# RWKV stage of a two-block kernel: the finished outputs in one part behind the second first inverse on VectorE, the first low rank weights loaded during the projection, and the first tile's own order

## The reference, cut to what matters

```python
def rwkv7_scan(r, w, k, v, kk, a, S):
    """S_t = S_{t-1} (diag(w_t) - kk_t^T (a_t * kk_t)) + v_t^T k_t ;  y_t = S_t r_t."""

# rwkv_project
lw = einsum("zblr,zrd->zbld", tanh(einsum("bld,zdr->zblr", xw, w1)), w2) + w0
decay = exp(-exp(-softplus(-lw) - 0.5))
a = sigmoid(a0 + (xa @ a1) @ a2)
g = sigmoid(xg @ g1) @ g2
kk = k * kvec[0] / max(sqrt(sum over the head of (k * kvec[0])^2), 1e-12)
k = k * (1 + (a - 1) * kvec[1])

# rwkv_out
y = head_layernorm(y, lnx[0], lnx[1])
bonus = sum over the head of (r * k * kvec[2]) * v
return ((y + bonus) * g) @ w_o
```

## Time and profile before

| | us |
|---|---|
| median of 3 runs | 3209.08 (3206.1 to 3211.09) |
| the profiled execution, its own time | 3212.0 |
| its span, first to last instruction | 3210.0 |
| TensorE busy | 3044.9 (95%) |
| VectorE busy | 1132.0 (35%) |
| ScalarE busy | 586.4 (18%) |
| GpSimd busy | 230.5 (7%) |

### The profile page before, as it was taken

The page is one execution under the profiler, slowest core; times in us unless marked ns, Lnnn a source line. Parts: engine busy times, 40 slices in busy tenths (PEclk is TensorE's granted clock), DMA queues, the critical chain, the costliest instruction groups (busy, mean ns, idle before and its releaser), DMA issues. The chain is left out here.

```text
span 3210.0 us, 54308 instructions
## 1 busy us (share of the span) xinstructions
PE 3044.9 (95%) x24038; PEld 1845.4 (57%) x24038; DVE 1132.0 (35%) x2357; ACT 586.4 (18%) x1323; POOL 230.5 (7%) x202
## 2 busy tenths in 40 slices
PE   7999999899999999989987999999999799998998
PEld 5899884633333333344766444444554687887887
DVE  3455006201100110033065444421231776864650
ACT  1011013300000000022044200000111555442100
POOL 0000000100000000000022100000000323230000
PEclk9999999899999999989988999999999899998999
DMA  9846539489998899932001322333321100005430
GB/s 376 315 173 234 196 142 372 199 355 380 390 372 346 354 380 385 402 125 79 1 2 81 142 106 79 118 131 118 118 76 50 35 15 27 15 3 198 144 144 13
DMA packets 88492, 577.03 MB, mean 180 GB/s; under 512 B 9536, under 2 KB 15936, under 8 KB 20672
## 3 DMA queue, kind: packets, MB, share of 16 engines
q1 hardware_dynamic: 84800, 568.27, 45.3%
q10 hardware_dynamic: 3456, 5.24, 0.4%
HBM read 567.19 MB, written 6.29 MB: 179 GB/s over the span
## 5 line engine op out<-in xcount | busy, mean ns | idle before, releaser
L272 PE MATMUL ps<-H,ring 128*128 128x256 f32 (+1 forms) x2480 | 803.6, 486 | 12.6 <-PEq L3300 4.1
L272 PEld LDWEIGHTS ps<-H,ring 128*128 128x128 f32 x2480 | 477.8, 194 | 336.8 <-issue 296.6
L272 PE MATMUL ps<-W,ring 128*128 128x256 f32 (+1 forms) x1616 | 490.5, 465 | 9.1 <-DVE W L3133 4.1
L1962 PE MATMUL ps<-ring,W 128*32 128x512 f32 (+1 forms) x2816 | 461.4, 594 | 1.7 <-ACT H L2021 1.7
L272 PEld LDWEIGHTS ps<-W,ring 128*128 128x128 f32 x1616 | 307.1, 191 | 192.1 <-issue 166.8
L1962 PEld LDWEIGHTS ps<-ring,W 128*32 128x32 f32 (+1 forms) x2816 | 142.5, 123 | 306.7 <-issue 304.1
L1985 PE MATMUL ps<-ring,W 128*64 128x512 f32 (+1 forms) x1408 | 231.1, 594 | 0.0
L2252 DVE SCALAR_TENSOR_TENSOR W<-ps,vec,W 128x189 f32<-128x189 f32 (+3 forms) x396 | 173.2, 437 | 14.0
L3700 POOL TENSOR_TENSOR ring<-ring 128x512 f32<-128x512 f32 x96 | 131.4, 1388 | 417.6 <-DVE ring L3724 334.7
L1985 PEld LDWEIGHTS ps<-ring,W 128*64 128x64 f32 (+1 forms) x1408 | 70.9, 123 | 156.9 <-issue 156.9
L2070 DVE TENSOR_TENSOR H<-ps,H 128x256 f32<-128x256 f32 x66 | 28.0, 425 | 303.2 <-ACT H L2012 303.2
(11 more groups left out here) (464 smaller groups left out, 3173.4 us busy)
## 6 DMA issues: line engine op xcount, KB each, us to landing
ring<-weights SPq DMA_DIRECT2D x528, 1024.0 KB, 8.0
rkv<-W ACTq DMA_DIRECT2D x16, 256.0 KB, 2.0
ring<-rkv SPq DMA_DIRECT2D x8, 512.0 KB, 3.7
X<-tokens SPq DMA_DIRECT2D x2, 1024.0 KB, 9.0
ring<-rw_tiles SPq DMA_DIRECT2D x8, 256.0 KB, 2.6
rkv<-W ACTq DMA_DIRECT2D x8, 128.0 KB, 5.5
ring<-rkv SPq DMA_DIRECT2D x8, 128.0 KB, 4.0
out<-X SPq DMA_DIRECT2D x8, 128.0 KB, 1.9
```

What stands on the lines that cost most here:

```text
L272: mm = pe.matmul(out(o), lhsT=k.ring[:, k.slot(at), p * P:(p + 1) * P], rhs=rhs(kk), start=kk == 0 and not (shared_bank and o % 2), stop=k ...
L1962: mm = pe.matmul(ps[at:at + n, r, :], lhsT=moe.Hg[:, kt, FIRST * e + first:FIRST * e + first + n], rhs=w[e][:, kk * WIDE:(kk + 1) * WIDE], ...
```

## The change

Four things are done, all in the RWKV stage.

1. VectorE's `scaled_output` and `gated_output` become one function, `finished_output`. It runs for tile q - 1 behind `first_inverse(j, 1)`, ahead of level 1, and the subtraction of the mean of tile q moves there with it. ScalarE's Square of the differences moves from ahead of the first evictions of the transposed tiles to level 3, behind the root of the keys.
2. The low rank weights of tile 0 are loaded by SyncE in `stage_rwkv_project`, once that stage's second group of products is done, into a part of `W` (`first_low`). `wj` gets one buffer in `W` and one in the ring, `sq` moves to the ring, and the low rank weights count on semaphores of their own (`low_in`), so the tile's data counts 32 a turn and no longer 48.
3. The two blocks become one. VectorE's constants stand at the start of its stream, GpSimd and VectorE wait for the masks where they first use them, and SyncE issues the load of tile 1 behind the masks without waiting.
4. Tile 0's preparation is written out ahead of the loop, which now starts at 0. Its three low rank products go to banks 2, 0 and 1 and don't wait for sigmoids. ScalarE takes the gate out between the decays of the two directions; VectorE runs both scans first, then keys, negative keys, the first decayed keys, the bonus and the rest. It waits for the masks behind all that.

```diff
@@ stage_rwkv_project, SyncE
             refill(k, sp, unit_done, 14, ahead=14)
+            sp.wait_ge(k.mm.sem, k.mm.at(out_done[last[1]]))
+            sp.dma_start(first_low(k), k.a["rw_tiles"][0]).then_inc(k.low_in[0], 16)
@@ Scan
+        self.wj = [w(512), r(512)]
-        self.sq, self.sqd, self.tk = w(512), w(256), k.X[:, 6:8, CTX]
+        self.sq, self.sqd, self.tk = r(512), w(256), k.X[:, 6:8, CTX]
-        self.wj = two(lambda: r(512))
@@ stage_rwkv
+    LOW_BANK = ((2, 0, 1), (2, 2, 2))
...
-        sp.dma_start(sc.wj[b], k.a["rw_tiles"][j]).then_inc(tile_in[b], 16)
+        if j:
+            sp.dma_start(sc.wj[b], k.a["rw_tiles"][j]).then_inc(k.low_in[b], 16)
...
-            sp.wait_ge(sem["masks_in"], 16)
-
-        @block.vector
-        def _(dve):
-            dve.memset(k.reset[:, :], 1.0).then_inc(sem["set_up"], 1)
...
-    with nc.Block() as block:
@@ TensorE
-                    pe.wait_ge(tile_in[n % 2], 48 * (n // 2 + 1))
+                    pe.wait_ge(k.low_in[n % 2], 16 * (n // 2 + 1))
...
-                else:
+                elif n:
                     pe.wait_ge(sem["sigmoid"], 3 * n + i)
...
-            for j in range(-1, TILES + 2):
+            for i in range(3):
+                low(0, i)
+            key_squares(0)
+            gate(0)
+            bonus(0)
+            for j in range(TILES + 2):
@@ ScalarE
+            for i in range(3):
+                sigmoids(0, i)
+            key_squares(0)
+            act.wait_ge(sem["set_up"], 2)
+            key_factors(0)
+            key_roots(0)
+            decays(0, 0)
+            gate_out(0)
+            decays(0, 1)
...
-                if behind:
-                    act.wait_ge(sem["d"], q + 1)
-                    act.activation(sc.sqd, sc.d, ACT.Square).then_inc(sem["d_squares"], 1)
...
+                    if behind and l == 3:
+                        act.wait_ge(sem["d"], q + 1)
+                        act.activation(sc.sqd, sc.d, ACT.Square).then_inc(sem["d_squares"], 1)
@@ GpSimd
+            pool.wait_ge(sem["masks_in"], 16)
@@ VectorE
-            def scaled_output(q):
+            def finished_output(q):
                 dve.wait_ge(sem["root_d"], q + 1)
                 after(dve.reciprocal(sc.sqd, sc.sqd))
                 after(dve.scalar_tensor_tensor(sc.d, sc.d, sc.col(q, 6), sc.sqd, ALU.mult, ALU.mult))
-
-            def gated_output(q):
                 after(dve.scalar_tensor_tensor(sc.d, sc.d, sc.col(q, 7), sc.bv[q % 4], ALU.add, ALU.add))
                 dve.tensor_tensor(k.H[:, q, LAT], sc.d, sc.g[q % 4], ALU.mult).then_inc(sem["fin"], 1)
...
+            for z in range(2):
+                scan(0, z)
+            key_to_product(0)
+            unit_keys(0)
+            negative_keys(0)
+            decayed_a(0, 0)
+            bonus(0)
+            decayed_b(0, 0)
+            decayed_a(0, 1)
+            decayed_b(0, 1)
+            dve.wait_ge(sem["masks_in"], 16)
+            for j in range(TILES + 3):
...
                 next_state(s, 0)
-                if inside(q - 1):
-                    gated_output(q - 1)
-                if behind:
-                    dve.wait_ge(sem["mean"], q + 1)
...
                 if here:
                     first_inverse(j, 1)
+                if inside(q - 1):
+                    finished_output(q - 1)
+                if behind:
+                    dve.wait_ge(sem["mean"], q + 1)
+                    if q:
+                        dve.wait_ge(sem["fin"], q)
+                    dve.scalar_tensor_tensor(sc.d, ps[:, sc.Y, S:2 * S], -1.0 / CH, sc.y, ALU.mult, ALU.add).then_inc(sem["d"], 1)
...
-                    if behind and l == 5:
-                        scaled_output(q)
```

More of the change, by code:

```diff
@@ L159, in __init__ @@
         self.ctx_in, self.lat_in = nc.alloc_semaphore("rwkv_context_in"), nc.alloc_semaphore("rwkv_latents_in")
+        self.low_in = [nc.alloc_semaphore(f"rwkv_low_in_{i}") for i in range(2)]
         self.turns_over = nc.alloc_semaphore("second_slots_over")
@@ L3208, in __init__ @@
         self.BKR = two(lambda: w(1024).rearrange("p (h z i n) -> p h z i n", h=2, z=2, i=2))
+        self.wj = [w(512), r(512)]
+        assert self.wj[0].shape == first_low(k).shape and pools["W"][1] == LOW + 512
         self.G = two(lambda: w(16))
@@ L3619, in sigmoids, with key_squares, key_factors, key_roots @@
                 act.wait_ge(sem["low"], 3 * n + i + 1)
+                src = ps[:, LOW_BANK[n > 0][i], :]
                 if i == 0:
-                    act.activation(sc.a, ps[:, 2, :], ACT.Sigmoid, bias=sc.col(n, 2)).then_inc(sem["sigmoid"], 1)
+                    act.activation(sc.a, src, ACT.Sigmoid, bias=sc.col(n, 2)).then_inc(sem["sigmoid"], 1)
                 else:
-                    act.activation(chunks8(sc.s[i - 1])[:, :, 1:CH + 1], chunks8(ps[:, 2, :]), ACT.Sigmoid,
+                    act.activation(chunks8(sc.s[i - 1])[:, :, 1:CH + 1], chunks8(src), ACT.Sigmoid,
                                    bias=sc.col(n, i - 1)).then_inc(sem["sigmoid"], 1)
-            for j in range(-1, TILES + 2):
+            def key_squares(n):
+                act.wait_ge(tile_in[n % 2], 32 * (n // 2 + 1))
+                if n:
+                    act.wait_ge(sem["kk"], n)
+                act.activation(sc.sq, sc.rkv[n % 2][:, 1, :], ACT.Square, scale=sc.col(n, 3)).then_inc(sem["squares"], 1)
+            def key_factors(n):
+                act.wait_ge(sem["sigmoid"], 3 * n + 1)
+                act.activation(sc.tk, sc.a.rearrange("p (a t) -> p a t", a=2), ACT.Identity,
+                               scale=sc.col(n, 4), bias=sc.rest[:, n:n + 1]).then_inc(sem["tk"], 1)
+            def key_roots(n):
+                act.wait_ge(sem["sums"], n + 1)
+                act.activation(sc.sq, ps[:, 2, :], ACT.Sqrt).then_inc(sem["roots"], 1)
+            def gate_out(n):
+                act.wait_ge(sem["gate"], n + 1)
+                act.activation(sc.g[n % 4], ps[:, 2, 0:S], ACT.Copy).then_inc(sem["gate_out"], 1)
+            for i in range(3):
[7 more added lines that the diff above has]
+            decays(0, 1)
+            for j in range(TILES + 2):
                 s, q, n = j - 1, j - 2, j + 1
@@ L3664, in _ @@
                             sigmoids(n, 2)
[L3665 to L3670, removed]
+                            key_squares(n)
+                            key_factors(n)
                         elif l == 3:
-                            act.wait_ge(sem["sums"], n + 1)
-                            act.activation(sc.sq, ps[:, 2, :], ACT.Sqrt).then_inc(sem["roots"], 1)
+                            key_roots(n)
+                    if behind and l == 3:
+                        act.wait_ge(sem["d"], q + 1)
+                        act.activation(sc.sqd, sc.d, ACT.Square).then_inc(sem["d_squares"], 1)
                     if l == 4:
@@ L3678, in _ @@
                         if ahead:
-                            act.wait_ge(sem["gate"], n + 1)
-                            act.activation(sc.g[n % 4], ps[:, 2, 0:S], ACT.Copy).then_inc(sem["gate_out"], 1)
+                            gate_out(n)
                     if ahead and l > 3:
@@ L3704, in _ @@
         def _(dve):
+            dve.memset(k.reset[:, :], 1.0).then_inc(sem["set_up"], 1)
+            dve.wait_ge(sem["set_up"], 1)
+            for x in (k.reset[:, :], *sc.s):
+                dve.memset(chunks8(x)[:, :, 0:1], 0.0)
+            dve.memset(sc.eps, 64e-5)
+            for j in range(TILES):
+                ins = dve.tensor_scalar(sc.rest[:, j:j + 1], sc.col(j, 4), -1.0, 1.0, ALU.mult, ALU.add)
+            ins.then_inc(sem["set_up"], 1)
+            dve.wait_ge(sem["set_up"], 2)
             order = [0]
@@ L3765, in first_inverse, with bonus, negative_keys @@
                 dve.transpose(flat(sc.M[z]), flat(sc.MT[j % 2][z])).then_inc(sem["m0"], 1)
-            for j in range(-1, TILES + 3):
+            def bonus(n):
+                dve.wait_ge(sem["rest"], n + 1)
+                dve.tensor_tensor(sc.bv[n % 4], ps[:, 2, 0:S], sc.rkv[n % 2][:, 2, LAT], ALU.mult).then_inc(sem["bv"], 1)
+            def negative_keys(n):
+                after(dve.scalar_tensor_tensor(sc.ka2[:, 0, :], sc.kk, -1.0, sc.a, ALU.mult, ALU.mult))
+            for z in range(2):
[10 more added lines that the diff above has]
+            for j in range(TILES + 3):
                 s, q, n = j - 1, j - 2, j + 1
@@ L3811, in _ @@
                         elif l == 5:
[L3812 to L3814 removed]
+                            bonus(n)
+                            negative_keys(n)
                             decayed_a(n, 0)
[L3816 to L3817 removed]
                     if here:
```

19 lines of the change are left out of this document (6 added, 13 removed).

## The result

The changed kernel takes 3186.26 us (median of 6 runs, 3185.10 to 3187.58) against 3208.17 (6 runs, 3206.10 to 3211.09): ratio 0.9931, 95% interval 0.9918 to 0.9944, 21.9 us won. 3185.1 was predicted, with 3179 to 3195 as the range.

What follows compares the result with a forecast made beforehand. TensorE's fixed order of products was taken to bound middle tiles, so only its idle spots could be won. 10.6 + 6.6 + 5.4 + 5.2 - 1.6 - 2.2 = 24.0 us won gave 3185.1 us, range 3179 to 3195.

Steps and rivals of the forecast that it cites:

- First tile, 10.6 us: Start of tile 0: without the barrier and with overlapped low rank products, the first grams start 10.6 us earlier.
- Start of a tile, 1.32 us: Ahead of L3478 in tiles 3 to 7: the gated output's removal saves 1.32 us each, 6.6 in all; GpSimd stall stays.
- no wait over 0.5 us: Sign to check: TensorE has no wait over 0.5 us ahead of L3478's transposes in tiles 3 to 7.
- End of a tile, 1.03 us: Ends of tiles 2 to 6: TensorE's 1.03 us wait ahead of L3531 goes, 5.2 us in all.
- The new place: Ahead of level 1's additions: lateness costs 0 in tiles 3 to 6 and 1.6 us in tile 7.
- The clock, 5.4 us: Tiles 3 to 7: the five short half speed stretches go with TensorE's waits, winning 5.4 us.
- The tail, 2.2 us: Behind tile 7: tile 5's output between two steps of the chain of states makes it 2.2 us late.
- Nothing catches that up: In the tail: the 2.2 us of lateness in the chain of states was taken as lost in full.
- ScalarE, 0: The Square of the differences, 0.41 us, moved to level 3: costs 0, with no table load of its own.
- The first tile moved: Answers a rival: something else holds the first sigmoids back by 10 us, so the first tile doesn't move; 3195.7, chance 0.08.
- The clock rose: Answers a rival: TensorE stays at 1.2 GHz through tile 0, making the kernel slower, 3232 with one whole tile; chance 0.03.
- (a): Rival: the new place costs, half speed stretches stay (5.4 us) and turns with GpSimd come out worse (3.0); 3193.5, chance 0.17.

Runs made afterwards that it cites:

- the scale at level 5 again: Changed kernel with reciprocal and scale of the output back at level 5, gate and mean at the new place: 3190.12 us, ratio 0.9944 to the kernel before.
- before again: The unchanged kernel before, profiled once more: 3202.55 us in one run.
- first tile alone: Changed kernel with the outputs put back in two parts at their old places, leaving only the first tile's edits: 3200.91 us, ratio 0.9977 to the kernel before.
- whole output early: Changed kernel with the whole finished output and the mean ahead of the second masked grams: 3203.19 us, ratio 0.9982 to the kernel before.
- weights held back: Kernel before with the next stage's 11 weight transfers held back until the last output is done: 3207.00 us, one run.
- the later comparison: Changed kernel unaltered, profiled and timed again against the kernel before: 3187.51 us against 3206.97, ratio 0.9943.

## Why the prediction was right, and where it was not

- **First tile, 10.6 us: right.** From the projection's last product to the first grams 27.21 became 16.20, 11.0 us, by the steps written (Square at 2483.47, root done at 2486.80, then 7.73 us of VectorE). The sum took the head sums at half speed; the clock fell only at 2485.6, at full speed they took 1.12.
- **Start of a tile, 1.32 us: right.** 12.25 us without a stretch became 10.93, 1.32, and the stall beside GpSimd went to L3830 as said. The sign "no wait over 0.5 us" held in all of tiles 3 to 7 but tile 5, where 0.8 is left.
- **End of a tile, 1.03 us: right, a little small.** 1.16 a tile (the scale at level 5 again).
- **The new place: right.** Level 1's additions were late in tiles 3 to 6 and TensorE didn't notice. In tile 7 the start gained 1.33 us and the tile still lost 0.17 without a stretch (42.44 to 42.61), so the place cost 1.5; 1.6 was put down.
- **The clock, 5.4 us: the step failed.** It took the five short stretches of one profile as made by the waits, and so as won for certain. The second profile of the same kernel has all the waits and no stretch. What the runs show is weaker. In eight profiles with the new place and no wait at a tile's end, none of tiles 3 to 6 has a stretch. In five more profiles with a wait at the start or the end of a tile, none, two, two, four and none of them have. (These are, in order: before again, first tile alone, scale at level 5, whole output early, weights held back; the first profile of before had four too.) So the waits allow the stretches but don't force them; that none come without the waits rests on these few profiles. The Trainium skill (TensorE: Matmul & The Clock Gate, "Part 1: The HAM clock gate") says that the window over which the gate looks at TensorE runs freely, and that the same kernel therefore differs from run to run; the two profiles of before agree, with five stretches and none. The size was right for the one profile: its five stretches cost 5.7 us. But tile 7's stretch stayed and tile 0 got a new one in the first profile after, 2.5 us together, so the clock was worth about 3.2 between the two first profiles, and nothing between the two second ones. How much of it is in the medians is open.
- **Tile 0: missing.** A stretch behind a wait of 1.93 us at level 4, which both kernels have, cost 1.1 us in the first profile after and not in the second.
- **The tail, 2.2 us: the mechanism right, the term wrong.** The step grew by 2.15 us, as said. But "Nothing catches that up" was false: two waits of TensorE of 0.94 and 1.80 us, of which the prediction took no note though they stood in the trace as "issue", vanished. The likely reason is that the instructions had come in the meantime. The tail went from 28.55 to 28.62 us, and from 28.28 to 28.72 between the second profiles.
- **ScalarE, 0: right.** The moved Square brought no table load: 24 in the stage before and after.

24.0 us were forecast, 21.9 measured, and 19.5 in the later comparison. That the total came so close is in part luck, since the terms that failed go against each other: about 2 us too much cost in the tail, against a clock term that came only in part. None of the rivals happened as a whole. The first tile moved. The clock rose 8.2 us behind the first grams (7.3 before). Of (a) only a stretch in tile 7 is seen; the turns with GpSimd cost what was put down.

## What to carry to other kernels

Work that nothing waits for goes where its engine is idle for longer than it takes, and the length to count is the one with the port pair's turns: a product with two SBUF operands beside GpSimd took 1.4 us instead of 0.5. The same place isn't right in the prologue and the last turns of a pipeline, where the cover is missing; look at those turns by themselves. Before a stall is costed, one more profile of the same kernel tells which part of it belongs to the program, and waits on "issue" in a chain say that shortening another engine's step there may win nothing.

## What the runs showed of the hardware

- The same program at two profiles: five stretches of 3.4 us at 1.2 GHz in the RWKV tiles, or none. The tiles took 393.13 against 387.44 us.
- TensorE waited 0.9 to 1.2 and 1.8 us for nothing that another engine does, while 11 transfers of 1 MB filled the DMA engines; with these held back both waits were gone and the chain 3.1 to 3.4 us shorter. The two waits end 1.4 to 1.6 us behind the landing of 16 KB transfers of the instruction queue.
- VectorE's products with one operand in PSUM (L3844, L3873: 0.69 us), its transposes (0.71) and its reciprocal (1.71) ran at their usual length beside GpSimd in the changed kernel. Products with two SBUF operands were held up there: L3771 took 1.70 us (0.69 apart), L3830 1.52 (0.41), L3794 1.42 (0.485).
